# Filter transforms of a diffusion step: plain f32 products in place of split ones, all ten units' operands kept, the filter network on its own semaphore

## The reference, cut to what matters

```python
z = jnp.concatenate([t, jnp.cos(bands * w), -jnp.sin(bands * w)], axis=-1)
hid = jnp.sin(fr * (z @ w1 + b1))
hid = jnp.sin(fr * (hid @ w2 + b2))
filt = (hid @ w3).reshape(length, 2, HYENA_ORDER, D_HYENA) * window[:, None, None, :]
fwd, bwd = filt[:, 0], filt[:, 1]
two_sided = jnp.concatenate([fwd, zeros, bwd[1:][::-1]], axis=0)
two_sided = two_sided / jnp.sum(jnp.abs(two_sided), axis=0, keepdims=True)
return jnp.fft.rfft(two_sided, axis=0)
```

## Time and profile before

| | |
|---|---|
| runs | 3432.54, 3440.22, 3439.83 us; median 3439.83 |
| profiled execution | 3434.03 us, span 3432.1 us |
| filters, from the start to the projection's first instruction | 351.66 us |
| busy over the span | PE 3190.5 us (93%), DVE 2245.4 (65%), ACT 1697.3 (49%), POOL 397.4 (12%) |
| granted TensorE clock, mean | 0.959 |

### The profile page before, as it was taken

The page is one execution under the profiler, slowest core; times in us unless marked ns, Lnnn a source line. Parts: engine busy times, 40 slices in busy tenths (PEclk is TensorE's granted clock), DMA queues, the critical chain, the costliest instruction groups (busy, mean ns, idle before and its releaser), DMA issues.

```text
span 3432.1 us, 54507 instructions
## 1 busy us (share of the span) xinstructions
PE 3190.5 (93%) x22416; PEld 2468.7 (72%) x22416; DVE 2245.4 (65%) x2850; ACT 1697.3 (49%) x2194; POOL 397.4 (12%) x326
## 2 busy tenths in 40 slices
PE   4879799979899894999999999999999999999996
PEld 2546688868787783777777777777777777777774
DVE  6765423247766637777777777777777777777766
ACT  2222422136511322666666666666666666666664
POOL 1320010011155032000000000000000000000010
PEclk8789899989999996999999999999999999999998
DMA  3455262245378424677877787788778777777785
GB/s 133 162 188 188 102 164 87 79 126 141 142 267 277 144 92 166 261 284 288 294 277 287 278 295 276 272 296 288 275 289 296 273 291 293 275 292 274 277 332 199
DMA packets 226036, 791.15 MB, mean 231 GB/s; under 512 B 28526, under 2 KB 35322, under 8 KB 221565
## 3 DMA queue, kind: packets, MB, share of 16 engines
q1 hardware_dynamic: 206028, 722.02, 57.0%
q0 software_dynamic: 19760, 65.65, 6.7%
HBM read 730.31 MB, written 57.26 MB: 229 GB/s over the span
## 4 chain that ended last, share of the span: by engine, by line
PE 58%; DMA 1%; DVE 1%; ACT 0%; issue 0%; POOL 0%; SPq 0%; ACTq 0%; POOLq 0%; DVEq 0%
PE exp_bank L2860 15%; PE exp_bank L2862 14%; PE exp_bank L2861 14%; PE exp_bank L2870 14%; PE exp_bank L2842 1%; DMA out_y<-exp_xb 1%; PE exp_bank L2844 1%; DMA exp_xb<-residual 0%; PE exp_bank L2828 0%; DVE g_pick L2423 0%; DVE g_pick L2422 0%; DVE g_pick L2425 0%; DVE exp_lo L2556 0%; DMA exp_xq<-hidden_rows,g_rows_q 0%; PE exp_bank L2832 0%
## 5 line engine op out<-in xcount | busy, mean ns | idle before, releaser
L2556 DVE TENSOR_TENSOR exp_lo<-exp_raw,exp_hi 128x1024 fp32r<-128x1024 f32 x1056 | 1277.0, 1223 | 251.2 <-ACT exp_hi L2552 193.6
L2552 ACT ACTIVATE exp_hi<-exp_raw 128x1024 fp32r<-128x1024 f32 x1056 | 1119.4, 1062 | 570.7 <-PE exp_bank L2862 558.0
L2860 PE MATMUL exp_bank<-exp_hi,exp_xt 128*128 128x512 f32 (+1 forms) x1536 | 588.8, 383 | 1.6 <-DVE exp_xt L2709 1.0
L2862 PE MATMUL exp_bank<-exp_hi,exp_xt 128*128 128x512 f32 (+1 forms) x1536 | 572.1, 372 | 0.0
L2861 PE MATMUL exp_bank<-exp_lo,exp_xt 128*128 128x512 f32 (+1 forms) x1536 | 571.7, 372 | 0.0
L2860 PEld LDWEIGHTS exp_bank<-exp_hi,exp_xt 128*128 128x128 f32 x1536 | 289.5, 189 | 87.5 <-issue 39.1
L2862 PEld LDWEIGHTS exp_bank<-exp_hi,exp_xt 128*128 128x128 f32 x1536 | 289.8, 189 | 52.0
L2870 PE MATMUL exp_bank<-exp_raw,exp_xtp 128*32 128x256 f32 (+1 forms) x6144 | 324.1, 363 | 0.0
L2861 PEld LDWEIGHTS exp_bank<-exp_lo,exp_xt 128*128 128x128 f32 x1536 | 290.3, 189 | 45.5
L2860 PE MATMUL exp_bank<-exp_hi,exp_hid 128*128 128x512 f32 x704 | 283.3, 402 | 10.4 <-DVE exp_lo L2556 10.4
L2870 PEld LDWEIGHTS exp_bank<-exp_raw,exp_xtp 128*32 128x32 f32 x6144 | 185.1, 110 | 127.0 <-issue 30.9
(11 more groups left out here) (414 smaller groups left out, 4568.6 us busy)
## 6 DMA issues: line engine op xcount, KB each, us to landing
exp_raw<-in_w SPq DMA_DIRECT2D x1056, 512.0 KB, 6.5
hy_table<-in_basis_s POOLq DMA_DIRECT2D x64, 512.0 KB, 4.7
carry_tiles<-in_w_ada SPq DMA_DIRECT2D x24, 1024.0 KB, 5.4
proj_raw<-in_w_in SPq DMA_DIRECT2D x24, 512.0 KB, 4.6
filt_raw<-in_kbasis_s SPq DMA_DIRECT2D x18, 512.0 KB, 6.1
spectrum_s<-filt_spec SPq DMA_DIRECT2D x34, 256.0 KB, 2.2
carry_flex<-spectrum_s SPq DMA_DIRECT2D x16, 512.0 KB
features<-proj_xr SPq DMA_DIRECT2D x12, 512.0 KB, 3.0
```

What stands on the lines that cost most here:

```text
L2552: act.activation(st.hi[:, n % st.ns, :], raw(n), ACT.Copy).then_inc(st.hi_done, 1)
L2556: dve.tensor_tensor(st.lo[:, n % st.ns, :], raw(n), st.hi[:, n % st.ns, :].bitcast(F32), ALU.subtract).then_inc(st.lo_done, 1)
L2860: pe.matmul(out, xh, wh, start=(k == 0), stop=False)
L2862: mm = pe.matmul(out, xl, wh, start=False, stop=(k == nk - 1))
```

## The change

- **Products.** The transform multiplies plain f32 table by plain f32 operand: one matmul instruction for each table tile in place of three. The split of the table (`Stream`: ACT `split_hi`, DVE `split_lo`) and of the operands (`operand`, `low`) is gone; the table tiles land in four buffers and are used as they are.
- **Operands.** `opnd` has a slot for each of the ten units. Units 5 to 9 are generated between the jobs (0,1,j) of order 0, at j = 0, 3, 6, 9, 12, with their sums two jobs later; before, 5 to 7 stood there and 8 and 9 around the short jobs of order 1. POOL makes three of a unit's four operands, DVE the fourth (`odd_sine`).
- **Network.** Its six inputs have a semaphore of their own, `s_net`, and are issued first. The two halves of the 1024 sample columns stand on the two halves of the partitions (`hidden_s`), so DVE and ACT run over 512 columns. Only the upper half of `hid` is made in layer 1; the low part is formed from it.
- **Weights W1, W2.** Their sums and the low part move from DVE to POOL; the zero half of W2 is written by ACT.
- **Modulation steps.** The three that stood in the network part on PE come later.

```diff
-            for b in range(2):
-                sp.dma_start(w2[:, 64 * x:64 * x + 64], a["filt_w2"]).then_inc(s_in, 16)
...
+            for x in range(2):
+                sp.dma_start(w2[64 * x:64 * x + 64, :], a["filt_w2"]).then_inc(s_net, 16)
...
-                    bh, bl = st.tile(st.hi, c, ti), st.tile(st.lo, c, ti)
-                    pe.matmul(pk[n % 2][:], bh, opnd_h[:, at, x, :], start=(t == 0), stop=False)
-                    pe.matmul(pk[n % 2][:], bh, opnd_l[:, at, x, :], start=False, stop=False)
-                    mm = pe.matmul(pk[n % 2][:], bl, opnd_h[:, at, x, :], start=False, stop=(t == nt - 1 and not rank1))
+                    mm = pe.matmul(pk[n % 2][:], table[:, c % NR, ti * 128:(ti + 1) * 128], opnd[:, at, x, :],
+                                   start=(t == 0), stop=(t == nt - 1 and not rank1))
...
-            pe.wait_ge(s_in, 16 * 16)
-            hidden(0, (0, 1, 2))
-            ada(2)
-            hidden(1, (0,))
-            hidden(1, (1, 2))
-            ada()
-            gen(0)
+            pe.wait_ge(s_net, 16 * 6)
+            hidden_p(0)
+            hidden_s(0)
+            hidden_p(1)
+            hidden_s(1)
+            pe.wait_ge(s_in, 16 * 9)
+            gen(0)
+            ada()
             gen(1)
+            ada()
             sums(0)
             middles()
             close(0)
-            ada()
+            ada(2)
             gen(2)
...
+            def hidden_s(layer):
+                for h in range(2):
+                    rows, out = slice(64 * h, 64 * h + 64), pf[1 + layer][64 * h:64 * h + 64, :]
+                    if layer:
+                        pe.wait_ge(s_sin, 2)
+                        mm = pe.matmul(out, w2[rows], hid[rows, ZS:ZS + 512], start=True, stop=True)
+                    else:
+                        mm = pe.matmul(out, w1[:], z[:, ZS + 512 * h:ZS + 512 * h + 512], start=True, stop=True)
+                mm.then_inc(s_h, 1)
...
         def _(pool):
+            pool.wait_ge(s_w3, 32)
+            pool.tensor_tensor(wsum[:, :, 0, :], w3[:, 0], w3[:, 1], ALU.add).then_inc(s_ws, 1)
+            pool.tensor_tensor(wsum[:, :, 1, :], w3[:, 1], w3[:, 0], ALU.subtract).then_inc(s_ws, 1)
+            pool.wait_ge(s_wh, 1)
+            pool.tensor_tensor(W2[0:64], wsum[0:64], W1[0:64].bitcast(F32), ALU.subtract).then_inc(s_wl, 1)
...
+            def odd_sine(n):
+                dve.wait_ge(s_AB, 2 * n + 2)
+                dve.tensor_tensor(opnd[:, n, 3, :], AB[:, 2, :], AB[:, 3, :], ALU.add).then_inc(s_diff, 1)
```

More of the change, by code:

```diff
@@ L892, in filters @@
     with Phase(nc, "filt") as ph:
-        st = Stream(ph, 3, 2, ph.sem("chunk_used"))
-        w1, w2 = ph.sb("w1", [33, 64]), ph.sb("w2", [64, 128])
+        table = ph.sb("table", [128, NR, CH])
+        s_tab, s_used = [ph.sem(f"table_landed{b}") for b in range(NR)], ph.sem("table_used")
+        w1, w2 = ph.sb("w1", [33, 64]), ph.sb("w2", [128, 64])
         fb = ph.sb("fb", [128, 3])
@@ L1245, in _ @@
         def _(act):
-            act.wait_ge(s_in, 16 * 16)
-            act.activation(sgn[:], sgn_f[:], ACT.Copy)
+            act.wait_ge(s_cond, 16)
             act.activation(sc[:], cond[:], ACT.Silu).then_inc(s_silu, 1)
[L1249 to L1259, removed]
+            for part, (rows, c0, c1) in enumerate(((64, ZP, ZS), (128, ZS, ZS + 512))):
+                act.wait_ge(s_y, part + 1)
+                act.activation(hid[0:rows, c0:c1], y[0:rows, c0:c1], ACT.Sin).then_inc(s_sin, 1)
+            act.wait_ge(s_ws, 2)
+            act.activation(W1[:], wsum, ACT.Copy).then_inc(s_wh, 1)
+            act.activation(W2[64:128], wsum[64:128], ACT.Copy, scale=0.0).then_inc(s_wz, 1)
+            act.wait_ge(s_y, 3)
+            act.wait_ge(s_h, 3)
+            act.activation(hid[0:64, ZP:ZS], y[0:64, ZP:ZS], ACT.Sin).then_inc(s_sin, 1)
+            act.wait_ge(s_sin, 3)
+            act.activation(hs[0:64, ZP:ZS], hid[0:64, ZP:ZS], ACT.Copy).then_inc(s_hh, 1)
+            act.wait_ge(s_y, 4)
+            act.wait_ge(s_h, 4)
+            for h in range(2):
+                c0 = ZS + 512 * h
+                act.activation(hid[0:64, c0:c0 + 512], y[64 * h:64 * h + 64, ZS:ZS + 512], ACT.Sin).then_inc(s_sin, 1)
+            for h in range(2):
+                c0 = ZS + 512 * h
+                act.wait_ge(s_sin, 4 + h)
+                act.activation(hs[0:64, c0:c0 + 512], hid[0:64, c0:c0 + 512], ACT.Copy).then_inc(s_hh, 1)
+            act.wait_ge(s_in, 16 * 9)
+            act.activation(sgn[:], sgn_f[:], ACT.Copy).then_inc(s_sin, 1)
             def absolute(n):
@@ L1267, in absolute @@
                     else:
-                        act.wait_ge(s_hl, 2)
+                        act.wait_ge(s_hl, 3)
                         act.wait_ge(s_AB, 2)
                     act.activation(out, AB[:, 2 * s:2 * s + 2, :], ACT.Abs).then_inc(s_abs, 1)
[L1272 to L1282, removed]
             def x_square(t):
@@ L1358, in reduced @@
             def reduced(layer, part):
[L1359 to L1369 removed]
+                np_, c0, c1 = ((64, ZP, ZS), (128, ZS, ZS + 512))[part]
+                bank = pf[1 + layer if part else 0]
+                yy, kx = y[0:np_, c0:c1], kk[0:np_, c0:c1]
+                dve.wait_ge(s_h, 2 * layer + part + 1)
+                if layer:
+                    dve.wait_ge(s_sin, part + 1)
+                else:
+                    dve.wait_ge(s_h, 2)
+                chain(dve.tensor_scalar(yy, bank[0:np_, 0:c1 - c0], fb[0:np_, layer:layer + 1], fb[0:np_, 2:3], ALU.add, ALU.mult))
                 chain(dve.tensor_scalar(kx, yy, 1.0 / (2 * np.pi), MAGIC, ALU.mult, ALU.add))
@@ L1468, in _ @@
             ada()
-            windowed(2)
-            low(1)
-            larger(2)
+            unit(2)
             ada()
```

231 lines of the change are left out of this document (74 added, 157 removed).

## The result

The changed kernel takes 3485.51 us (median; 3480.98 to 3488.51) against 3439.77 of the kernel before on the same chip, a ratio of 1.0137 with a 95% interval of 1.0119 to 1.0155. It is slower by about 46 us; 3411 was forecast, and the range ended at 3436. The profiled execution has a span of 3485.4 us, and the projection begins at 400.00 us instead of 351.66: 48.3 of the 53.3 us by which the span grew lie in the filters.

What follows compares the result with a forecast made beforehand. TensorE bounds the long jobs; in start and passage it waits for VectorE chains. Terms -17.6 + 0.7 + 7.9 - 29 + 13 = -25 us on 3434.0 give 3409, forecast as 3411 for the median; range 3389 to 3436.

Steps and rivals of the forecast that it cites:

- start: Up to the first generation: early small loads, halved columns and weights on GpSimd cut 46.15 to 28.5 us, -17.6.
- first units: First five units, middle samples, short jobs of order 0: saved splits offset by serial modulation turns, 86.3 to 87 us, +0.7.
- long jobs, order 0: Dearer products +10.5, an extra unit +5.1, less 8 of idle and half clock: 97.1 to 105 us.
- passage: Between the orders: operand splits, waits and two units go, five short jobs and two modulation steps remain; 43.0 to 14 us.
- long jobs, order 1: Products +10.5, a seventh modulation step +1.4, half-clock opening +3.4, store waits -2: 71.0 to 84 us.
- The sign that the prediction had set for itself: The forecast is wrong if the long-job stretches of both orders together grow by more than 45 us.
- Rival B: Gain given back: late units between long jobs cost 37 us, or GpSimd starves at the start; 3436 or 3435, chance 0.14.
- the arm that bounds it: In the start, the weights' arm, mainly 4096 columns on GpSimd in 10.2 to 18.2 us, ending at 23.4 to 31.
- The products: In long jobs, a plain product takes 0.853 us against 0.70 for three split ones, +10.5 us in each order.
- opening at half clock: First long job of order 1 runs its eight records at double length behind the passage's waits, +3.4 us.
- Rival C: Long-job plain products run at 1.2 GHz, each 0.853 us dearer; half of them make +58 us, 3469; chance 0.08.

Runs made afterwards that it cites:

- run 1: The changed kernel with VectorE making two modulation copies instead of one behind unit 0's reciprocal, so its copies run one step ahead; 3405.74 us, ratio 0.9925.
- run 4: run 1's kernel with the weights' sums and low part back on VectorE, GpSimd doing nothing in the start; 3401.89 us, ratio 0.9913.
- run 3: The kernel before with each table tile's three split products replaced by one plain f32 product of the high parts; 3440.07 us, ratio 1.0028.
- run 5: run 4's kernel with the first three modulation steps each moved one place earlier on TensorE and VectorE; 3394.27 us, ratio 0.9892.

## Why the prediction was wrong

By its own steps, in us of the profiled executions; "run 1" is the changed kernel without the lag:

| stretch | before | forecast | changed | run 1 |
|---|---|---|---|---|
| start | 46.2 | 28.5 | 30.9 | 30.8 |
| first units | 86.3 | 87 | 95.8 | 81.1 |
| long jobs, order 0 | 97.1 | 105 | 149.2 | 100.4 |
| passage | 43.0 | 14 | 18.3 | 17.0 |
| long jobs, order 1 | 71.0 | 84 | 97.6 | 78.4 |
| projection begins | 351.7 | 326 | 400.0 | 316.0 |

- **The step that failed** is the costing of the two long-job stretches. It priced a modulation step at its 1.41 us of work and asked of VectorE only whether it had time enough. For the first units it named which copy each step needs; it stopped counting there, and the four steps of TensorE against three copies of VectorE behind the first close stand in the change. With the lag the two stretches came out 44 and 14 us above the forecast; without it, in run 1, 4.6 and 5.6 below. The sign that the prediction had set for itself, more than 45 us of growth in the two together, came: 78.7.
- **The first units** are the same error: +9.5 for a forecast +0.7, and -5.2 in run 1, inside the bounds given.
- **Rival B** foresaw 37 us from waits at each unit between long jobs, put before the sums as in the earlier trace rows. In the changed kernel TensorE never waits there (no wait of a sum L1153 is in its list); it waits at the modulation steps, and in order 1 too, where B had nothing. Its price, which ended at no change, was too low.
- **The start** was right to 2.4 us; the arm that bounds it was not. GpSimd took 2.62 + 2.51 + 4.60 = 9.7 us for the weights, just under the lower bound of 10.2, and was done at 26.9. VectorE's chain ended at 30.3, since it was the one that stood still (below); with GpSimd out of the way in run 4 it ended at 24.9, ahead of the weights' low part.
- **The products** were right per instruction (0.853 forecast), and +10.5 in each order was too much: run 3 shows -2.3 in order 0, +8.1 in order 1. In order 1 the +3.4 for an opening at half clock was too much as well: in run 1 the first job's products took 4.2 us, not twice 3.4. Rival C is refuted: 0.99 to 1.00 of the clock in runs 1 and 5.
- **The passage**: 14 for 17.0 to 18.3. The 14 was the old length of a stretch of five short jobs (14.76), and the two modulation steps had no term. In run 1 the five jobs took 10.7 us and the steps 6.3; the steps ran at half the clock, behind TensorE's waits for the scalings of the short jobs (1.01 + 1.89 us each).

Without the one word the forecast of 3411 would have been 3 us off: run 1's ratio puts 3439.8 at 3414. That closeness is in part luck. Run 1's projection begins at 316.0, 10.7 us ahead of the 326.7 that the forecast's terms give; but the rest of the program, which no edit touches, took 3088.4 us in its profiled execution against 3080.4 in that of the kernel before. Over the eleven profiled executions that rest varies from 3080 to 3088 us, so gains of a few us are better read from the filters than from the whole.

## What to carry to other kernels

Where two engines run lists written by hand, count on both what is issued up to each meeting point, and do it again behind every place that the change touches: a step that is one ahead on one side turns a wait for something done long ago into a wait for the engine's whole local queue. An engine that is idle for more than half of a stretch, as VectorE in order 0 of the changed kernel (61.55 us busy of 149.18), can still be the one that is waited for; look for a short instruction behind long ones. And small steps without a deadline belong where the waiting engine idles anyway (run 5), not where they are next in number.

## What the runs showed of the hardware

In the start of the changed kernel three instructions of VectorE that read and wrote 512 columns of SBUF stood still until the instruction of GpSimd that had begun before them was over (they ended 0.3 to 0.6 us behind it), while GpSimd lost nothing: its eight pieces of 512 columns took 9.7 us, and alone they would take 10.2 at 1.27 each. VectorE and then GpSimd:

```profile
23.31 3.85 DVE L1349 TENSOR_SCALAR filt_kz<-filt_opnd 128x512 f32<-128x512 f32 x1
27.19 0.43 DVE L1350 TENSOR_SCALAR filt_kz<-filt_kz 128x512 f32<-128x512 f32 x1
```

```profile
22.27 4.60 POOL L1309 TENSOR_TENSOR filt_W<-filt_AB,filt_W 64x2048 fp32r<-64x2048 f32 x1 [5.00 <-ACT filt_W L1252]
```

GpSimd's instruction ended at 26.87, the one-input step of VectorE at 27.16, and the next like it took 0.43 us. Two others were held in the same way (L1350, 2.44 us; the first of three L1352, 2.71 us, the three together 4.16). In run 4, where GpSimd does nothing in the start, the same steps took 0.43, 0.43 and 2.14 us. So VectorE lost about 7.4 us in all, against 4.7 that the same work costs it when it does it itself. A step of VectorE that began at the same moment as GpSimd's first instruction (12.17) was not held, 0.43 us. Elsewhere it is GpSimd that is slowed, 2.27 us for a piece of 1.27.

The prediction took VectorE as the one that disturbs and GpSimd as the one that is slowed, and weighed only instructions of two inputs. The Trainium skill (SBUF — State Buffer, SBUF: two separate sides) says that GpSimd shares a port pair with those instructions of VectorE that run in a 2-port mode or have two SBUF inputs, that the pair is locked exclusively, and that the one that starts first has it for its whole instruction while the other is fully blocked. The 3.85 against 0.43 us agrees; in which mode this one-input instruction ran, the trace does not tell.
